# The first three weight units of a decoder layer, one block at a time, and x turned behind the products

## The reference

```python
hn = rms_norm(x, norm_mix)                       # x: 256 x 2048
q, k, v = jnp.split(hn @ w_in, 3, axis=-1)       # w_in: 2048 x 6144
q, k = rms_norm per head of 128, with gains
y = stick_breaking_attention(q, k, v) @ w_out
x = x + y
x = x + (silu(h @ w_gate) * (h @ w_up)) @ w_down  # h = rms_norm(x, norm_ffn), d_ff 5632
gate = sigmoid(rms_norm(x, ple_norm) @ ple_w_gate)
x = x + gate * (p @ ple_w_proj)
```

## Time and profile before

| | |
|---|---|
| Median of 3 runs | 1246.95 us (1246.75 to 1247.27) |
| Profiled execution: own time | 1247.0 us |
| Profiled execution: span, first to last instruction | 1245.3 us |
| TensorE matmul busy | 1236.6 us (99%) |
| VectorE, ScalarE, GpSimd busy | 702.6, 623.2, 77.9 us |
| Weights and inputs read | 226.78 MB, 184 GB/s over the span |
| Share of TensorE in the chain that ended last | 98% |
| First product of the layer starts at | 11.09 us |

### The profile page before, as it was taken

How to read it: one execution, slowest core, us unless ns; L and a number is a source line. 1 busy time by engine, 2 the same in 40 slices (tenths; PEclk the granted TensorE clock), 3 DMA queues, 4 the chain that set the end, 5 groups by cost and what they waited for, 6 DMA issues and landing times.

```text
span 1245.3 us, 17289 instructions
## 1 busy us (share of the span) xinstructions
PE 1236.6 (99%) x5688; PEld 1028.3 (83%) x5688; DVE 702.6 (56%) x778; ACT 623.2 (50%) x752; POOL 77.9 (6%) x126
## 2 busy tenths in 40 slices
PE   9999999999999999999999999999999999999998
PEld 7888888888888888888888888888888788888886
DVE  6667566675765654555555555455545455545554
ACT  5458486684954544444444444444444444444443
POOL 0312103021000200000000000000000000002000
PEclk9999999999999999999999999999999999999999
DMA  7655555545455666666666666666565656565574
GB/s 262 203 166 160 164 174 163 184 152 163 152 179 184 185 194 193 186 187 185 198 188 188 187 185 194 189 187 186 181 203 174 193 181 208 165 210 161 195 216 137
DMA packets 120462, 229.24 MB, mean 184 GB/s; under 512 B 7490, under 2 KB 9844, under 8 KB 120436
## 3 DMA queue, kind: packets, MB, share of 16 engines
q1 hardware_dynamic: 119252, 226.80, 59.2%
q10 hardware_dynamic: 1184, 2.11, 0.5%
HBM read 226.78 MB, written 2.10 MB: 184 GB/s over the span
## 4 chain that ended last, share of the span: by engine, by line
PE 98%; issue 1%; DVE 0%; ACT 0%; DMA 0%; SPq 0%; ACTq 0%; DVEq 0%
PE acc L903 93%; PE T L917 2%; PE T L931 1%; PE Z L931 1%; PE R L954 1%; DMA x<-in_x 0%; ACT w_hi L389 0%; PE acc L1015 0%; PE Z L944 0%; DVE w_lo L621 0%; PE R L955 0%; DVE stage L867 0%; DVE x L870 0%; DVE neg_log_1m L674 0%; ACT softplus L448 0%
## 5 line engine op out<-in xcount | busy, mean ns | idle before, releaser
L621 DVE TENSOR_TENSOR w_lo<-raw,w_hi 128x1024 fp32r<-128x1024 f32 (+1 forms) x448 | 528.9, 1189 | 413.6 <-ACT w_hi L389 411.6
L389 ACT ACTIVATE w_hi<-raw 128x1024 fp32r<-128x1024 f32 (+1 forms) x448 | 455.5, 1020 | 547.2 <-PE acc L903 521.2
L903 PE MATMUL acc<-w_hi,xT_hi 128*128 128x512 f32 x1216 | 477.8, 393 | 0.0
L903 PE MATMUL acc<-w_hi,xT_lo 128*128 128x512 f32 x1216 | 473.9, 390 | 0.0
L903 PE MATMUL acc<-w_lo,xT_hi 128*128 128x512 f32 x1216 | 473.2, 389 | 0.0
L903 PEld LDWEIGHTS acc<-w_hi,xT_lo 128*128 128x128 f32 x1216 | 228.2, 188 | 48.1
L903 PEld LDWEIGHTS acc<-w_lo,xT_hi 128*128 128x128 f32 x1216 | 228.5, 188 | 46.1
L903 PEld LDWEIGHTS acc<-w_hi,xT_hi 128*128 128x128 f32 x1216 | 228.4, 188 | 45.9 <-ACT stage L586 0.2
L903 PE MATMUL acc<-w_hi,hT_hi 128*128 128x512 f32 x352 | 137.5, 391 | 0.5 <-DVE w_lo L621 0.5
L903 PE MATMUL acc<-w_hi,hT_lo 128*128 128x512 f32 x352 | 137.0, 389 | 0.0
L903 PE MATMUL acc<-w_lo,hT_hi 128*128 128x512 f32 x352 | 137.0, 389 | 0.0
(11 more groups left out here) (121 smaller groups left out, 654.7 us busy)
## 6 DMA issues: line engine op xcount, KB each, us to landing
raw<-in_sb_w_in SPq DMA_DIRECT2D x96, 512.0 KB, 3.7
raw<-in_ffn_w_gate SPq DMA_DIRECT2D x88, 512.0 KB, 3.7
raw<-in_ffn_w_up SPq DMA_DIRECT2D x88, 512.0 KB, 3.7
raw<-in_ffn_w_down SPq DMA_DIRECT2D x80, 512.0 KB, 4.8
raw<-in_sb_w_out SPq DMA_DIRECT2D x32, 512.0 KB, 4.1
raw<-in_ple_w_gate SPq DMA_DIRECT2D x20, 512.0 KB, 5.1
raw<-in_ple_w_gate SPq DMA_DIRECT2D x24, 256.0 KB, 3.3
raw<-in_ffn_w_down SPq DMA_DIRECT2D x16, 256.0 KB, 3.1
```

The lines of the kernel that those rows point to most:

```text
L389: act.activation(w_parts[0][:, slot(u), 0:n, :], raw[:, slot(u), 0:n, :], ACT.Copy).then_inc(hi_ready, 1)
L621: dve.tensor_tensor(w_parts[1][:, slot(u), 0:n, :], raw[:, slot(u), 0:n, :], w_parts[0][:, slot(u), 0:n, :].bitcast(F32), ALU.subtract).th ...
L903: last = pe.matmul(acc[pair][tb][:, :], parts[a][:, c, tb * P:(tb + 1) * P], w_parts[w][:, slot(u), i, :], start=(start and i == 0 and n = ...
```

## The change

Four edits, all in group 0 of the attention part:

- Units 0 to 2 (`SPLIT`) are loaded as two DMAs of one block each, split one block at a time by ScalarE and VectorE, and multiplied one block at a time (`first_products`).
- The two blocks of round 0 of x are turned into two different banks (`T[0]` and `R`) with a signal each, and scaled and split one at a time. The fillers are now 10 ahead of the gains, 2 behind them, and 2 between round 0 and round 1.
- TensorE turns round u+2 of x behind the products of unit u, not ahead of them, in all of units 0 to 6.
- The last half of x is loaded as whole 128x512 pieces, and VectorE's eight sums of squares stand in units 3 to 10, not 1 to 8.

```diff
-WARM = 4, 9
+WARM = 10, 2, 2
+SPLIT = 3
@@ SyncE
             for u in range(DU):
-                load(A0 + u, u, D_UNITS[u], w_in[:, 0:NT])
-                if u == 0:
-                    load_x(1)
-                if u + 2 < DU:
-                    load_x(u + 2)
+                if u < SPLIT:
+                    load_half(u, 0, half_landed[u])
+                    if u == 0:
+                        load_x(1)
+                    load_half(u, 1, landed[slot(u)])
+                    if u > 0:
+                        load_x(u + 1)
+                else:
+                    load(A0 + u, u, D_UNITS[u], w_in[:, 0:NT])
+                    if u - 1 < XN:
+                        load_x_tile(u - 1)
@@ ScalarE
+            def first_units(u):
+                if u == 0:
+                    act.wait_ge(block_turned, 1)
+                    act.activation(xT[0][:, 0, :], T[0][:, 0, :], ACT.Copy, scale=gains[:, MIX:MIX + 1]).then_inc(block_hi_ready, 1)
+                else:
+                    turn_x(u)
+                act.wait_ge(half_landed[u], 16)
+                act.activation(w_parts[0][:, slot(u), 0, :], raw[:, slot(u), 0, :], ACT.Copy).then_inc(half_hi_ready, 1)
+                if u == 0:
+                    act.wait_ge(T_ready, 1)
+                    act.activation(xT[0][:, 1, :], R[:, 0:SEQ], ACT.Copy, scale=gains[:, MIX + 1:MIX + 2]).then_inc(turned_hi, 1)
+                act.wait_ge(landed[slot(u)], 16)
+                act.activation(w_parts[0][:, slot(u), 1, :], raw[:, slot(u), 1, :], ACT.Copy).then_inc(hi_ready, 1)
@@ VectorE
+            def first_units(u):
+                if u == 0:
+                    dve.wait_ge(block_hi_ready, 1)
+                    turn_block(0, MIX, 0, 0).then_inc(block_ready, 1)
+                else:
+                    dve.wait_ge(turned_hi, u + 1)
+                    turn_block(2 * u, MIX, u % 2, 0)
+                    turn_block(2 * u + 1, MIX, u % 2, 1).then_inc(T_free[u % 2], 1)
+                dve.wait_ge(half_hi_ready, u + 1)
+                half_lo(u, 0).then_inc(half_lo_ready, 1)
...
+                dve.wait_ge(hi_ready, u + 1)
+                half_lo(u, 1).then_inc(lo_ready, 1)
...
-                    if first and 1 <= u <= DU:
-                        t, tb = (u - 1) // 2, (u - 1) % 2
+                    if first and SPLIT <= u < SPLIT + XN * TB:
+                        t, tb = (u - SPLIT) // 2, (u - SPLIT) % 2
@@ TensorE
+            def first_products(u):
+                for i, c in enumerate(D_UNITS[u]):
+                    if i == 0:
+                        pe.wait_ge(half_lo_ready, u + 1)
...
+                    for tb in range(TB):
+                        for n, (a, w) in enumerate(TERMS):
+                            last = pe.matmul(acc[0][tb][:, :], xT[a][:, c, tb * P:(tb + 1) * P], w_parts[w][:, slot(u), i, :],
+                                             start=(u == 0 and i == 0 and n == 0), stop=False)
+                last.then_inc(unit_used, 1)
...
-                        if u + 2 < X_ROUNDS:
-                            turn_input(u + 2)
...
-                    products(U0 + u, u, xT, D_UNITS[k], part % 2, k == 0, k == DU - 1, before)
+                    if first and u < SPLIT:
+                        first_products(u)
+                    else:
+                        products(U0 + u, u, xT, D_UNITS[k], part % 2, k == 0, k == DU - 1, before)
+                    if first and u + 2 < X_ROUNDS:
+                        turn_input(u + 2)
...
-            turn_input(0)
+            keep_busy(WARM[1])
+            pe.wait_ge(x_loaded[0], 16)
+            for k, to in enumerate((T[0][:, 0, :], R[:, 0:SEQ])):
+                for tb in range(TB):
+                    last = pe.transpose(to[:, tb * P:(tb + 1) * P], x[:, tb, k * P:(k + 1) * P], ident[:, :])
+                last.then_inc(T_ready if k else block_turned, 1)
+            keep_busy(WARM[2])
             turn_input(1)
-            keep_busy(WARM[1])
```

More of the change, by code:

```diff
@@ L173, in trunk @@
         unit_used = sem("unit_used")
+        half_landed = [sem(f"half_landed{u}") for u in range(SPLIT)]
+        half_hi_ready = sem("half_hi_ready")
+        half_lo_ready = sem("half_lo_ready")
+        block_turned = sem("block_turned")
+        block_hi_ready = sem("block_hi_ready")
+        block_ready = sem("block_ready")
         half_done = sem("half_done")
@@ L474, in group @@
                 for u in range(AU):
+                    if first and u == 0:
+                        act.wait_ge(gains_ready, 1)
+                    if first and u < SPLIT:
+                        first_units(u)
+                        continue
                     if first and u < DU:
-                        act.wait_ge(gains_ready, 1)
                         turn_x(u)
@@ L636, in turn_tile, with half_lo @@
                     turn_block(t * CB + 2 * b + 1, gain, b, 1).then_inc(T_free[b], 1)
+            def half_lo(u, i):
+                return dve.tensor_tensor(w_parts[1][:, slot(u), i, :], raw[:, slot(u), i, :],
+                                         w_parts[0][:, slot(u), i, :].bitcast(F32), ALU.subtract)
+            def first_units(u):
[8 more added lines that the diff above has]
+                half_lo(u, 0).then_inc(half_lo_ready, 1)
+                if u == 0:
+                    dve.wait_ge(turned_hi, 1)
+                    dve.scalar_tensor_tensor(out=xT[1][:, 1, :], in0=R[:, 0:SEQ], scalar=gains[:, MIX + 1:MIX + 2],
+                                             in1=xT[0][:, 1, :].bitcast(F32), op0=ALU.mult, op1=ALU.subtract).then_inc(T_free[0], 1)
+                dve.wait_ge(hi_ready, u + 1)
+                half_lo(u, 1).then_inc(lo_ready, 1)
             def sum_heads(n):
@@ L980, in turn_input @@
                 if r < KD // 2:
-                    pe.wait_ge(x_loaded[r], 16)
+                    for half in ((r,) if r < KD // 4 else (r - r % 2, r - r % 2 + 1)):
+                        pe.wait_ge(x_loaded[half], 16)
                     turn(r % 2, x, 2 * r, r // 2)
```

18 lines of the change are left out of this document (16 added, 2 removed).

## The result

| | before | changed |
|---|---|---|
| Median of 8 runs | 1247.11 us (1246.47 to 1248.36) | 1250.86 us (1249.81 to 1252.32) |
| Ratio | | 1.0029, 95% interval 1.0018 to 1.0040 |
| Profiled execution: own time, span | 1247.0, 1245.3 us | 1250.38, 1248.4 us |

The changed kernel is slower by 3.75 us, 0.3%, and its interval lies, but for its first 0.02%, beyond the 0.2% that the prediction calls no change. The profiled executions differ by 3.1 us in span and 3.4 in own time.

The account below looks back on a forecast made before the run. TensorE, busy 99% of the span, was taken as the bound. Terms -2.2 + 0.45 + 0.3 + 5.8 + 1.5 = +5.85 us on 1247.0 gave 1252.8 us, range 1250.3 to 1254.7.

Parts of the forecast that it names:

- part 1: Start of the kernel: the first product starts at 8.9 us and not at 11.09, a gain of 2.2 us.
- parts 1 to 3: Up to unit 7: start -2.2, round 2 of x behind the first product +0.45, x turned later +0.3; 1.45 us earlier.
- part 4: Sums of squares end 7.3 us behind unit 7's first product, so `normed` is late and TensorE waits: +5.8 us.
- hole: TensorE's idle time ahead of the turn of `normed`, forecast at 5.8 us, some 45.7 to 51.5 us.
- part 5: Behind TensorE's idle time ahead of `normed`: pace halves for 3.0 us, +1.5 us, though the granted clock's column says 0.
- part 3: Units 3 to 7: x turned later makes TensorE wait some 0.2 us in about every second unit, +0.3 us.
- Full pace behind the hole: Rival: TensorE idles ahead of `normed` but keeps full pace afterwards; 1251.35 us, chance 0.27.
- The small hole: Rival: VectorE catches up, only the ring holds the last sum; TensorE waits 1.6 us ahead of `normed`; 1247.2 us, chance 0.07.
- no hole: Rival: last sum ends within 1.5 us of unit 7's start, so the lead stays; 1245.6 us, chance 0.08.
- The start gains nothing: Rival: first products at half pace or halves land late, the 1.45 us lead goes, TensorE still idles; 1254.3 us, chance 0.08.

Follow-up runs that it names:

- experiment 5: Changed kernel with 22 filler matmuls (44 passes) ahead of TensorE's wait for `normed`: 1249.72 us, ratio 1.0014.
- experiment 7: Kernel before with four one-element ScalarE activations, at the start of its program: 1246.06 us, ratio 0.9987; at its end: 1247.54 us, ratio 1.0001.
- experiments 1 and 2: 1: kernel before with the sums in units 3 to 10, 1249.62 us; 2: changed kernel with x turned ahead again from unit 2, 1246.32 us.
- experiments 2 to 4: Changed kernel; 2: x turned ahead from unit 2, 1246.32 us; 3: sums in units 1 to 8, 1246.87, or 0 to 7, 1245.36; 4: x ahead, sums 0 to 7, 1243.87.
- experiment 4: Changed kernel with x turned ahead again from unit 2 and the sums in units 0 to 7: 1243.87 us, ratio 0.9972.

## Why the prediction was right

It had said slower, 1252.8 us with a range of 1250.3 to 1254.7; the time is 1250.86, 0.56 above the lower end. The mechanism is the one forecast. By its own steps, relative to the kernel before:

| term | forecast | measured |
|---|---|---|
| first product (part 1) | -2.2 | -2.31 |
| parts 1 to 3: unit 7 | -1.45 | -1.36 |
| end of the last sum behind unit 7 (part 4) | 7.3 | 7.15 |
| from there to `normed` written | 12.1 | 11.0 |
| hole (part 4) | 5.8 | 4.75 |
| pace behind it (part 5) | 1.5 | 1.14; 1.26 by experiment 5 |
| stops of ScalarE | none | -1.45; -1.50 by experiment 7 |
| sum | +5.85 | +3.1 in span, +3.75 in medians |

**Parts 1 to 3** hold within 0.1 us in sum, with some luck. The passes of filler ran at half pace as taken (0.21 us), and the chain of x, `w_hi` and `w_lo` had its old lengths; but part 1's 0.1 us is less than the start moves between executions (8.66 to 9.61 with this start). Of the waits in units 3 to 7 two came, at every second unit, 0.5 us together for the 0.3 of part 3.

**Part 4** was right in its count of VectorE's work, 7.15 for 7.3, and experiments 1 and 2 confirm that both the place of the sums and the later x are in it. Its mis-sized term is GpSimd's chain, put at 4.35 + 0.1 + 6.36 = 10.8 us from the earlier trace rows; it took 9.7, counted from the sum's end as there (39.24 to 48.95). Four kinds of its small instructions are short or long by about one microsecond: `pair_sum` took 0.20 for 1.11, the two `head_ms` 0.51 for 1.41, the two `head_scale` 0.63 for 1.69, but two steps of `newton` 1.06 and 1.04 us where they had taken 0.20 and 0.19 (at 36.80 and 37.08 us). Together that is -1.16 us. The long ones of the changed kernel, at 41.64 and 42.78, lie beside VectorE's three `w_lo` of 40.29 to 43.78; the short ones at 44.56 and 48.32 lie in VectorE's own wait, and the short one at 39.33 beside the head sums (39.16), an instruction with one input. Before, the long ones at 33.57, 38.46 and 43.13 likewise lie beside a `w_lo`, which VectorE ran from 33.40, 38.27 and 43.10. So the chain shortened itself by 2.0 us in `head_ms` and `head_scale`: while the hole is open VectorE has nothing to run. What decides is whether an instruction starts inside a `w_lo`: those at 33.57, 41.64 and 42.78 end 0.04 to 0.06 us behind the `w_lo` that they started in, and the one of 0.72 us at 40.16, which started 0.13 ahead of one, has its old length. The Trainium skill (GPSIMD Engine Reference, Specifications) states that GpSimd shares its way to SBUF with VectorE and is held up by VectorE's instructions with two SBUF inputs; `w_lo` has two, and the traces agree: an instruction that is caught near the start of a `w_lo` takes 0.9 us longer.

**Part 5** sided with the passes against the granted clock's column, rightly: behind 4.75 us without work TensorE ran at half pace for 3.0 us, until 53.30. The column read 0.50 in this case; at the very start it reads 1.00 beside passes at half pace, so it can't be trusted there. The term was 0.2 to 0.4 us too large: it took half of the 3.0 us for lost, but the six products from 51.04 to 53.30 took 2.26 us for some 1.37 (six by 0.228), and the transposes lost some 0.2.

**What was not foreseen**, and is the largest single difference: the stops of ScalarE, a term that the prediction put at nothing. They are in the chain of the kernel before, at 978 and 1183 us, far from the change, and its page sums them up as "issue 1%". The prediction read only the first 80 us of the chain. The range was made for the start and the pace; the 1.45 us here and the 1.05 by which the hole came out smaller, both outside what it was made for, took the time almost to its end, so that it held is in part luck.

**The rivals.** "Full pace behind the hole" (1251.35) is closest in time to the result and is ruled out by the trace: the pace did halve. The small hole and no hole are ruled out by `pair_sum`, 7.24 us behind unit 7; they are what experiments 2 to 4 make of the changed kernel. "The start gains nothing" is ruled out by 8.78 us and by experiment 4.

The spans account for 3.1 us; own time adds 0.3 and the medians another 0.4, and for neither is a cause known.

## What to carry to other kernels

Before small work is moved later in an in-order queue, count in rows all the work that stands ahead of it there and the whole chain that hangs on it: eight sums of 0.69 us, moved two units back behind an x that is turned one unit later, cost more than a start shortened by 2.3 us gave, since 10 us of GpSimd work begin with the last of them. The kernel with the split start, x turned ahead and the sums first keeps the gain and is 3.69 us, 0.3%, faster than before, 1.5 of them by the stops of experiment 7. And where a fraction of a per cent is measured, run the old kernel with a few idle instructions at the start as a control: a shift of ScalarE's program alone was worth 1.5 us here.

## What the runs showed of the hardware that was not expected

- ScalarE was idle for 1.2 to 4.3 us in the middle of its work with no releaser, and each time a packet of a DMA queue of the kind "instruction" had ended 0.9 to 1.2 us before it went on. Where this happens depends on the position of the code in its program: four instructions ahead moved the stops to where TensorE does not have to wait (-1.50 us), four behind did nothing.
- TensorE kept its pace behind 0.8, 2.17 (twice) and 2.46 us without work, and lost it behind 4.75 us (1.14 to 1.26 us in time) and, at the start, behind 3.02 us, where it took some 6 us to come back.
- A GpSimd instruction on 128x4 values takes 0.20 us alone and 1.1 us when it starts just inside a `w_lo` of VectorE: it ends with that `w_lo`. So the length of a chain there depends on what VectorE does meanwhile, by 1.1 us in 10.8.
